# The last two gate tiles of a decoder trunk, done on one half of the tokens and then on the other

## What is computed

```python
gate = jax.nn.sigmoid(rmsnorm(h, norm_ple_w[i]) @ w_pg[i])
h = h + ((p[i] @ w_ple[i]) * gate).astype(h.dtype)
return rmsnorm(h, final_norm_w)
```

```python
y = xf * lax.rsqrt(jnp.mean(xf * xf, axis=-1, keepdims=True) + EPS) * w.astype(jnp.float32)
```

## Time and profile before

| | us |
|---|---|
| median of 3 runs | 2256.48 (2256.35 to 2256.61) |
| profiled execution, own time | 2258.48 |
| its span | 2256.8 |
| PE busy in it | 2225.9 (99%) |
| DVE busy | 1395.4 (62%) |
| ACT busy | 839.5 (37%) |
| POOL busy | 329.5 (15%) |
| mean bandwidth of DMA | 115 GB/s |

### The profile page before, as it was taken

The page is one execution under the profiler, slowest core; times in us unless marked ns, Lnnn a source line. Parts: engine busy times, 40 slices in busy tenths (PEclk is TensorE's granted clock), DMA queues, the critical chain, the costliest instruction groups (busy, mean ns, idle before and its releaser), DMA issues.

```text
span 2256.8 us, 32877 instructions
## 1 busy us (share of the span) xinstructions
PE 2225.9 (99%) x13224; PEld 1965.5 (87%) x13224; DVE 1395.4 (62%) x1561; ACT 839.5 (37%) x954; POOL 329.5 (15%) x293
## 2 busy tenths in 40 slices
PE   9999999999999999999999999999999999999997
PEld 7787877888888899999999999999888888888886
DVE  7476235453358998888888888886333333336444
ACT  6222235542243444444444444444222222226433
POOL 5992004000000111111111111110000000000001
PEclk9999999999999999999999999999999999999999
DMA  6322221124433322333223333235333332232222
GB/s 217 127 73 94 98 94 61 57 88 159 146 110 117 118 109 115 125 125 125 110 103 121 125 125 125 100 149 218 113 118 125 117 121 94 93 120 94 104 100 75
DMA packets 59018, 260.13 MB, mean 115 GB/s; under 512 B 6320, under 2 KB 15152, under 8 KB 38608
## 3 DMA queue, kind: packets, MB, share of 16 engines
q1 hardware_dynamic: 55440, 247.81, 30.6%
q0 software_dynamic: 3520, 11.54, 1.3%
HBM read 237.30 MB, written 22.02 MB: 115 GB/s over the span
## 4 chain that ended last, share of the span: by engine, by line
PE 88%; POOL 6%; DVE 3%; issue 1%; ACT 1%; DMA 1%; SPq 0%; DVEq 0%; POOLq 0%; ACTq 0%
PE bank L643 28%; PE bank L641 28%; PE bank L642 28%; DVE w_lo L1814 1%; PE bank L743 1%; DVE xs_lo L1469 1%; PE bank L823 0%; DMA Y<-in_x 0%; PE bank L818 0%; DVE xs_lo L1471 0%; PE bank L807 0%; POOL QKV L2119 0%; PE bank L677 0%; POOL QKV L2116 0%; DVE Y L2016 0%
## 5 line engine op out<-in xcount | busy, mean ns | idle before, releaser
L641 PE MATMUL bank<-x_block_hi,w_hi 128*128 128x256 f32 x2240 | 631.7, 282 | 4.1 <-DVE u_two L1837 1.6
L643 PE MATMUL bank<-x_block_hi,w_lo 128*128 128x256 f32 x2240 | 631.9, 282 | 0.0
L642 PE MATMUL bank<-x_block_lo,w_hi 128*128 128x256 f32 x2240 | 629.2, 281 | 0.0
L1035 ACT ACTIVATE w_hi<-w_raw 128x2048 fp32r<-128x2048 f32 (+1 forms) x134 | 222.5, 1660 | 746.5 <-PE bank L643 746.5
L641 PE MATMUL bank<-xs_hi,w_hi 128*128 128x512 f32 x1152 | 456.8, 397 | 4.7 <-DVE xs_lo L1471 1.9
L642 PE MATMUL bank<-xs_lo,w_hi 128*128 128x512 f32 x1152 | 449.8, 390 | 0.0
L643 PE MATMUL bank<-xs_hi,w_lo 128*128 128x512 f32 x1152 | 449.8, 390 | 0.0
L641 PEld LDWEIGHTS bank<-x_block_hi,w_hi 128*128 128x128 f32 x2240 | 426.0, 190 | 5.4 <-DVE w_lo L1814 3.2
L642 PEld LDWEIGHTS bank<-x_block_lo,w_hi 128*128 128x128 f32 x2240 | 426.2, 190 | 0.0
L643 PEld LDWEIGHTS bank<-x_block_hi,w_lo 128*128 128x128 f32 x2240 | 425.7, 190 | 0.0
L1448 DVE TENSOR_TENSOR w_lo<-w_raw,w_hi 128x2048 fp32r<-128x2048 f32 (+1 forms) x136 | 270.6, 1990 | 109.4 <-ACT w_hi L1035 106.7
(11 more groups left out here) (324 smaller groups left out, 2557.5 us busy)
## 6 DMA issues: line engine op xcount, KB each, us to landing
w_raw<-in_w_up SPq DMA_DIRECT2D x48, 1024.0 KB, 5.1
w_raw<-in_w_down SPq DMA_DIRECT2D x64, 704.0 KB, 4.1
Y<-in_w_up SPq DMA_DIRECT2D x40, 1024.0 KB, 6.3
w_raw<-in_w_in SPq DMA_DIRECT2D x31, 1024.0 KB, 4.8
w_raw<-in_w_out SPq DMA_DIRECT2D x16, 1024.0 KB, 4.9
w_raw<-in_w_pg SPq DMA_DIRECT2D x16, 1024.0 KB, 4.7
mid_kept<-val POOLq DMA_DIRECT2D x44, 256.0 KB, 2.3
mid_raw<-mid_kept SPq DMA_DIRECT2D x15, 512.0 KB, 5.1
```

The lines of the kernel that those rows point to most:

```text
L641: nc.tensor.matmul(out, w_h, x_h, start=first, stop=False, skip_group_check=onto)
L642: nc.tensor.matmul(out, w_h, x_l, start=False, stop=False, skip_group_check=onto)
L643: return nc.tensor.matmul(out, w_l, x_h, start=False, stop=last, skip_group_check=onto)
L1035: nc.scalar.activation(w_hi[c % 2][:, 0:width], w_raw[c % 2][:, 0:width], ACT.Copy).then_inc(hi_made, 1)
```

## The change

The loops stop at tile 13 (`FULL = KT - 2`). Tiles 14 and 15 are then done on tokens 0 to 255 (half 0) and again on tokens 256 to 511 (half 1): 192 matmuls of 256 columns on PE instead of 96 of 512, with half 1 in banks 3 and 4. The scale, sigmoid, product, sum, square and, for tile 14, the adding to `ss` are done per tile and half. Within PE's work on half 1 stand two insertions: the sums of squares of half 0 at k = 10 of tile 14, and the spread of half 0's norm at k = 3 of tile 15. The root, the refinement and the diagonal are done per half. All 16 tiles are multiplied by the norm and written out per half: 32 transfers of 128 KB in rows of 1 KB instead of 16. The ten idle matmuls stand only in half 1's sum, the nine behind it. ACT's block of 14 scalings stays where it was.

SP:

```diff
-            for t in range(KT):
+            for e in range(2):
+                for t in range(KT):
...
+                    if from_pool:
+                        sp.wait_ge(out_pool_made, POOL_OUT * e + j + 1)
+                    else:
+                        sp.wait_ge(out_made, (KT - POOL_OUT) * e + j + 1 - POOL_OUT)
+                    sp.dma_start(A["out"][:, j, tokens(e)], Y[:, j, tokens(e)]).then_inc(written, 16)
```

PE:

```diff
+            def sum_half(e, warm):
+
+                pe.wait_ge(sq_used, 3 * KT + FULL + e + 1)
+                blocks = (2 * e, 2 * e + 1)
+                for j in blocks:
+                    nc.tensor.matmul(bank[2][:, j:j + 1], ss[:, j * P:(j + 1) * P], ones[:, 0:1], start=j == blocks[0],
+                                     stop=False, skip_group_check=True)
+                for _ in range(warm):
+                    nc.tensor.matmul(bank[7][:, 0:P], ones[:], ident[:], start=True, stop=True)
+                pe.wait_ge(squared, 3 * KT + FULL + 2 * e + 2)
+                for j in blocks:
+                    m = nc.tensor.matmul(bank[2][:, j:j + 1], sq[:, j * P:(j + 1) * P], ones[:, 0:1], start=False,
+                                         stop=j == blocks[1], skip_group_check=True)
+                m.then_inc(sum_spread, 1)
+
+            def spread_half(e):
+
+                pe.wait_ge(diag_made, 3 + e)
+                for b in (6, 5) if e == 0 else (1, 0):
+                    nc.tensor.matmul(bank[b][:, tokens(e)], ones[:], val[:, tokens(e)], start=True,
+                                     stop=True).then_inc(rstd_spread, 1)
+
+            for e in range(2):
+                for s in range(2):
...
+                    for k in range(KT):
+                        if e == 1 and s == 0 and k == 10:
+                            sum_half(0, 0)
+                        if e == 1 and s == 1 and k == 3:
+                            spread_half(0)
+                        ks = slice(k * P, (k + 1) * P)
+                        last = product(out, w_hi[slot][:, ks], w_lo[slot][:, ks], xs_hi[:, k, tokens(e)],
+                                       xs_lo[:, k, tokens(e)], k == 0, k == KT - 1)
+                    last.then_inc(tile_done, 1)
+            sum_half(1, WARM_GATE)
             for _ in range(WARM_ROOT):
                 nc.tensor.matmul(bank[7][:, 0:P], ones[:], ident[:], start=True, stop=True)
...
+            spread_half(1)
```

ACT, behind its loop:

```diff
+            def gate_half(j, e):
+
+                u, hs = order(j, e), tokens(e)
+                act.wait_ge(evacuated, u + (PG0 - 2 + 1))
+                nc.scalar.activation(conv_acc[:, hs], conv_acc[:, hs], ACT.Sigmoid).then_inc(gate_made, 1)
+                act.wait_ge(h_made, u + 1)
+                act.wait_ge(sq_used, 3 * KT + FULL + e + j - FULL)
+                nc.scalar.activation(sq[:, hs], Y[:, j, hs], ACT.Square).then_inc(squared, 1)
...
+            for j in range(FULL):
                 scale_out(j)
...
+            gate_half(FULL, 0)
+            gate_half(FULL + 1, 0)
+            for j in range(FULL, KT):
+                scale_out(j, 0)
+            root_half(0)
+            gate_half(FULL, 1)
+            keep_rstd(0)
+            gate_half(FULL + 1, 1)
+            root_half(1)
+            for j in range(FULL, KT):
+                scale_out(j, 1)
+            keep_rstd(1)
```

DVE, behind its loop (`add_gated_half`, `rms_half` and `finish_half` are the former steps on 256 tokens; `finish_half` has the eleven products):

```diff
+            add_gated_half(FULL, 0)
+            add_gated_half(FULL + 1, 0)
+            rms_half(0)
+            add_gated_half(FULL, 1)
+            finish_half(0)
+            add_gated_half(FULL + 1, 1)
+            rms_half(1)
+            finish_half(1)
```

POOL:

```diff
+            for e in range(2):
+                pool.wait_ge(rstd_made, 4 + e)
+                for j in range(POOL_OUT):
+                    tt(Y[:, j, tokens(e)], Y[:, j, tokens(e)], rstd[:, tokens(e)],
+                       ALU.mult).then_inc(out_pool_made, 1)
```

More of the change, by code:

```diff
@@ L234, in build @@
         p_raw = [conv_acc[:], silu_g[:]]
+        FULL = KT - 2
         cos_t, sin_t = Y[:, 8, :], Y[:, 9, :]
@@ L466, in kv_place, with tokens, order @@
             return bank[(3, 4, 6, 2)[2 * (c % 2) + c // 4]][:, (c // 2 % 2) * DV:(c // 2 % 2 + 1) * DV]
+        def tokens(e):
+            return slice(e * HALF_T, (e + 1) * HALF_T)
+        def order(j, e):
+            return j if j < FULL else FULL + 2 * e + j - FULL
         block = ctx.enter_context(nc.Block())
@@ L627, in _ @@
                     weights(PG0 + s, i, A["w_pg"][2 * i + s], W_FULL)
-            for t in range(KT):
[L630 to L634, removed]
+            for e in range(2):
+                for t in range(KT):
+                    from_pool = t % 3 == 2 and t // 3 < POOL_OUT
+                    j = t // 3 if from_pool else POOL_OUT + t - min((t + 1) // 3, POOL_OUT)
+                    if from_pool:
[3 more added lines that the diff above has]
+                    sp.dma_start(A["out"][:, j, tokens(e)], Y[:, j, tokens(e)]).then_inc(written, 16)
+            sp.wait_ge(written, 32 * KT)
         @block.tensor
@@ L997, in _ @@
             spread_sum(3 * KT, ss[:], bank[2])
-            with pe.Fori(0, KT // 2) as i:
+            with pe.Fori(0, FULL // 2) as i:
                 for s in range(2):
@@ new lines, in spread_half @@
+            def spread_half(e):
[5 more added lines that the diff above has]
+                for s in range(2):
+                    if e == 0:
+                        pe.wait_ge(lo_made, FULL + (PG0 + s + 1))
+                        pe.wait_ge(evacuated, FULL + (PG0 - 2 + s - 1))
+                    slot = (PG0 + s) % 2
+                    out = bank[slot if e == 0 else 3 + s][:, tokens(e)]
+                    for k in range(KT):
[7 more added lines that the diff above has]
+                    last.then_inc(tile_done, 1)
@@ L1016, in _ @@
+            sum_half(1, WARM_GATE)
             for _ in range(WARM_ROOT):
                 nc.tensor.matmul(bank[7][:, 0:P], ones[:], ident[:], start=True, stop=True)
-            pe.wait_ge(diag_made, 3)
-            nc.tensor.matmul(bank[3][:], ones[:], val[:], start=True, stop=True).then_inc(rstd_spread, 1)
-            nc.tensor.matmul(bank[2][:], ones[:], val[:], start=True, stop=True).then_inc(rstd_spread, 1)
+            spread_half(1)
         @block.scalar
@@ L1404, in _, with gate @@
             root(2, rstd[:], val[:])
-            def gate(i, s, last):
+            def gate(i, s):
                 j = 2 * i + s
-                if not last:
-                    w_half(PG0 + 2 + s, i, used=2)
+                w_half(PG0 + 2 + s, i, used=2)
                 act.wait_ge(evacuated, j + (PG0 - 2 + 1))
@@ L1413, in gate @@
                 act.wait_ge(sq_used, j + 3 * KT)
-                src = Y[:, j, :] if isinstance(i, int) else Y[:, bass.ds(j, 1), :]
-                nc.scalar.activation(sq[:], src, ACT.Square).then_inc(squared, 1)
-            with act.Fori(0, KT // 2 - 1) as i:
+                nc.scalar.activation(sq[:], Y[:, bass.ds(j, 1), :], ACT.Square).then_inc(squared, 1)
+            with act.Fori(0, FULL // 2) as i:
                 for s in range(2):
[L1419 to L1423, removed]
@@ L1425, in _ @@
-            for j in range(KT - 2):
-                scale_out(j)
[L1427 to L1433, removed]
+                    gate(i, s)
+            def gate_half(j, e):
[5 more added lines that the diff above has]
+                nc.scalar.activation(sq[:, hs], Y[:, j, hs], ACT.Square).then_inc(squared, 1)
@@ new lines, in scale_out, with root_half, keep_rstd @@
+            def scale_out(j, e=None):
+                part = Y[:, j, :] if e is None else Y[:, j, tokens(e)]
+                act.wait_ge(squared, 3 * KT + order(j, e or 0) + 1)
+                nc.scalar.activation(part, part, ACT.Identity, scale=par("final", j)).then_inc(scaled, 1)
+            def root_half(e):
+                root(3 + e, norm4[:, 1, 2 * e:2 * e + 2], norm4[:, 0, 2 * e:2 * e + 2])
+            def keep_rstd(e):
+                act.wait_ge(rstd_spread, 3 + 2 * e)
+                nc.scalar.activation(rstd[:, tokens(e)], bank[(6, 1)[e]][:, tokens(e)], ACT.Copy).then_inc(rstd_made, 1)
@@ L1984, in _, with add_gated @@
             link(nc.vector.memset(ss[:], 0.0))
-            def add_gated(i, s, follow, square=True):
+            def add_gated(i, s):
                 j = 2 * i + s
@@ L1990, in add_gated @@
                 tt(conv_acc[:], bank[(PG0 + s) % 2][:], rstd[:], ALU.mult).then_inc(evacuated, 1)
[L1991 to L1997, removed]
+                w_rest(PG0 + 2 + s, i)
+                y, g = Y[:, bass.ds(j, 1), :], ple[:, bass.ds(j, 1), :]
+                v, gate = val[:].unsqueeze(1), conv_acc[:].unsqueeze(1)
                 dve.wait_ge(gate_made, j + 1)
@@ L2000, in add_gated @@
                 tt(y, y, v, ALU.add).then_inc(h_made, 1)
[L2001 to L2005, removed]
+                dve.wait_ge(h_made, j + 1)
+                add_square(j + 3 * KT)
+            with repeat(dve, FULL // 2, links=(links, 2)) as i:
```

(34 more changed lines are left out.)

3 lines of the change are left out of this document (removed).

## The result

The changed kernel takes 2261.29 us in the median of 15 runs (2259.46 to 2264.44), the kernel before, on the same chips, 2256.81 (15 runs, 2256.18 to 2258.3). The ratio is 1.0019, with a 95% interval of 1.0011 to 1.0026: 4.5 us, just under the 0.2% that was called no change, with an interval that reaches past it. The forecast was 2260.2 with a range of 2257.2 to 2262.8, worked out from the 2256.48 that three runs of the kernel before had shown.

A forecast was written before the change was run, and what follows sets the result against it. Bound by PE until 2234.45, then 9.5 us of serial chain and 12.7 of output. 2256.8 + 4.5 - 2.8 = 2258.5; the clock's +2.0 gives a span of 2260.5, 2260.2 for the median (+3.7 us), range 2257.2 to 2262.8.

The forecast's parts named there:

- the clock stays low: Rival: half clock lasts 6.8 us, nearly all under matmuls, costing 3.4; time 2261.6, +5.1, slower by 0.23%; chance 0.25.
- Matmuls, +1.1: Tiles 14 and 15 on PE: 192 matmuls of 256 columns instead of 96 of 512 add 1.1 us.
- The stop at k = 10, +5.0, of which 0.9 work: PE waits 2.4 and 1.6 us for half 0's squares, behind ACT's block of scalings; +5.0 us, 0.9 of it work.
- Sums and spread of half 0, +1.9 together: Insertions in PE's half 1 work: 0.9 us for the sums of squares at k = 10, 1.0 for the spread at k = 3.
- DVE's +0.4: The scale of tile 15, half 1, queues behind DVE's eleven half products of half 0: +0.4 us, staying with the lower clock.
- The clock, +2.0: PE's granted clock falls in or just behind the stop: floor 0, ceiling 3.4, taken as +2.0 us.
- The last chain, -2.8: From the last scale to the first issue, on halves: 6.7 us instead of 9.5, so -2.8, with 0.4 lost to a table load.
- The output, -2.8: Half 1's 16 transfers of 128 KB, issued 0.50 apart, end in 9.9 us instead of 12.7: -2.8.
- The table switches: Rival: each new ACT table switch takes its 1.28 us load twice; 1.3 us on the path, 2261.5; table or code, chance 0.09.
- PE doesn't stop: Rival: half 0's squares come in time at k = 10, 4.1 of the 5.0 go, clock holds; 2254.1; chance 0.06.

The follow-up runs named there:

- e4: The kernel before, with only the matmuls of tiles 14 and 15 done on 256 columns, all else whole; 2258.38 us, ratio 1.0004.
- e1: The changed kernel, with eight and five idle matmuls put into PE's two waits at k = 10; 2259.66 us, ratio 1.0010 to the kernel before.
- e2: The changed kernel, with the 14 scalings done by POOL instead of by ACT in one block; 2254.45 us, ratio 0.9988 to the kernel before.
- e3: The changed kernel, with each output tile written whole (16 transfers of 256 KB) once its half 1 is there; 2263.94 us, ratio 1.0030 to the kernel before.
- e5: The changed kernel, with the 14 scalings still on ACT but dealt out between the half gates; 2254.98 us, ratio 0.9988 to the kernel before.

## Why the prediction was right

The measured time lies inside the range, the shift has the sign that was forecast, and most terms hold one by one. The time alone doesn't decide for the forecast, though: 2261.29 is the upper end of its band, where that of "the clock stays low" begins, and 4.5 us lies between the 3.7 of the one and the 5.1 of the other. The terms decide. Against the runs:

- **Matmuls, +1.1.** 1.3 (e4).
- **The stop at k = 10, +5.0, of which 0.9 work.** The waits were read out of ACT's order and came as 2.26 and 1.54 (forecast 2.4 and 1.6). On PE the stop is worth 4.3 (e1 against e2), for the 4.1 left after the work.
- **Sums and spread of half 0, +1.9 together.** e2 against e4: 1.7.
- **DVE's +0.4.** It is there at full clock, in e1, where the last scale stands behind the products of half 0. The prediction wrote that it stays with the lower clock, "as its products shift too", and that was wrong: against e1 the products start 1.45 us later, while PE's end comes 2.3 later, and DVE waits 0.41 for PE (2242.54). This term was counted and is nothing in the changed kernel.
- **The clock, +2.0.** 2.3 on PE, for the forecast's 2.0 and the rival's 3.4. The price is near, but partly by luck. The forecast leaned to a lower stretch of 3.4 us, since 1.87 was the nearer wait; it lasted 6.8, as the rival had it. The price stayed low because 2.3 us of the stretch lay on the stop and the sums, and because a matmul at the lower clock took 1.8 times as long (0.213 against 0.119), not twice. The rival's 3.4 needs nearly all of the stretch under matmuls. Other executions end up to 3 us above the median, so the rival's price may be paid in some; no profile here caught one.
- **The last chain, -2.8.** From the last scale to the first issue 6.9 us, against 9.5: -2.6. The table load that comes out from under the sum shows as DVE's wait of 0.54 for the root, 0.27 before. ACT's half operations took 0.42, not 0.40.
- **The output, -2.8.** Issues from 2249.4 to 2257.0, 0.50 apart, landing in 1.8. e3, which undoes it, costs 2.7. By the 138 GB/s that the Trainium skill (DMA: Bandwidth & Descriptors, section "Measured (HBM→SBUF, 128 partitions, SWDGE, issued from GpSimd)") gives for 64 KB, the end would come some 6 us later than measured, an estimate from that page. The rows show 264 GB/s at 128 KB on one queue and 340 on two.
- **The table switches.** The root of half 0 starts 0.02 us behind its load (2231.38 + 1.28, then 2232.68), the sigmoid of (14, 1) in e5 as well, and in the changed kernel that sigmoid is released by DVE, 2 us after its load. The second part of a switch that the Trainium skill has (ScalarE: Activation LUTs, section "What ACT_TABLE_LOAD costs") doesn't show here either. Nor do the steps of half 0, which run first, take longer than those of half 1: ACT waits 0.95 us for the sum in each of the four half tiles.

On the way to the last scale, 1.3 + 1.7 + 4.3 + 2.3 on PE are the whole 9.6 us of its delay. That they add up is no proof, since each is the difference of two neighbouring kernels (one profiled execution each); what can be held against the prediction is each term by itself. From the common point the end moved by 4.2 where the forecast said 3.7: 0.2 more ahead of the last scale, 0.2 in the chain and 0.1 in the output. The median moved by 4.5; why it moved 0.3 more than the profiled execution is open.

"PE doesn't stop" was the rival on the faster side, at 2254.1. e2 and e5 made it true, at 2254.5 and 2255.0.

## What to carry to other kernels

When a step is split so that its first half can be used early, look at what each engine has written ahead of that half: a block that was free because it hid behind the unsplit step stands in front of it now. Deal the block out between the half's steps, or put it on an engine that is idle. And reckon an output's end by its pace of issue as well as by its bytes: half-size transfers paid where half of them could leave before the end, and cost 5 us where they couldn't.

## What the hardware showed beyond that

- Two waits of PE, 2.26 and 1.54 us, with a few matmuls of one column between, went with a granted clock of 0.50 for 6.8 us; it fell 0.1 us into the second wait. With waits of 0.48 and 0.32 and idle matmuls ahead of each (e1) it stayed at 1.00.
- At a granted clock of 0.50 the matmuls of 256 columns came 0.213 us apart, which is 256 columns at 1.2 GHz; at 1.00 they came 0.119 apart, where 256 columns at 2.4 GHz are 0.107. So the lower clock cost a factor of 1.8 here.
- One queue issued a transfer every 0.50 us whether its size was 128 KB or, until the DMA engines were full, 256 KB. Full meant 384 GB/s with rows of 2 KB and 340 with rows of 1 KB.
- A table load of 1.28 us was followed by its function within 0.02 to 0.04 us, for the root and for the sigmoid.
- POOL took 2.07 us to scale a tile of 512 columns by a value per partition, against 1.28 for a product of two tensors of that size in the kernel before. The trace of e2:

```profile
2218.55 2.07 POOL L2319 TENSOR_SCALAR Y<-Y,params_sb 128x512 f32<-128x512 f32 x1 [8.81 <-ACT sq L1454]
```
